# Split fp32r projections in the odd mixer of a two-layer diffusion backbone

## The reference, cut to what matters

```python
z = h @ w_in                                  # h: normed, modulated tokens
ux, ug, up = jnp.split(z, CD_SPLITS, axis=-1) # 512 columns each
zc = hc @ w_in[:, :LRU_W]                     # the context needs ux alone
xl = depthwise_conv(ux, conv_w, conv_b, LRU_PAD)
# for both directions: a, b from sigmoid gates of xl; h_lat += linear_scan(a, b, h0)
lat = [multiscale_pool(up, pool_w, pool_scale), h_lat * gelu(ug)]
x = x + mod[2] * merge_branches(lat, out_norm, w_out)
```

## Time and profile before

| | |
|---|---|
| median of 3 runs | 2559.59 us (2559.36 to 2560.53) |
| profiled execution, its own time | 2562.43 us |
| span of that execution | 2560.6 us |
| PE busy | 2239.7 us, 87% |
| DVE, ACT, POOL busy | 745.8, 606.8, 182.8 us |
| granted PE clock, mean | 0.924 of full speed |
| odd mixer, start of its block to the merge's | 1511.9 to 1788.8 us |
| PE's column sums in its norm (L545) | 1536.45 to 1540.87 us |
| first L490 of ACT in it | 1545.66 us |
| w_out loads of the merge | 4.19 MB, at about 390 GB/s |
| first product of the merge (L1252) | 1805.20 us |

### The profile page before, as it was taken

One profiled execution on the slowest core, in us unless ns is written; L12 is line 12 of the kernel. 1 busy time (PEld: TensorE's weight loads), 2 busy tenths in 40 slices (PEclk: granted clock), 3 DMA queues, 4 the chain that ended last, 5 costly groups with the idle time before them and its releaser, 6 DMA issues. The chain is left out here.

```text
span 2560.6 us, 34982 instructions
## 1 busy us (share of the span) xinstructions
PE 2239.7 (87%) x15176; PEld 1067.3 (42%) x15176; DVE 745.8 (29%) x1167; ACT 606.8 (24%) x960; POOL 182.8 (7%) x126
## 2 busy tenths in 40 slices
PE   4799998969997699999999738998995999988884
PEld 3577885534445233333333224443443333332222
DVE  3423226643114211111111183565315111111104
ACT  4421105541113111111111133554103111111111
POOL 0000000000000000000000021343000000000002
PEclk8799999988998899999999958999897999999986
DMA  8101108035661889889999450000105999999995
GB/s 329 41 25 33 42 2 335 1 91 205 213 214 52 348 358 414 355 346 414 417 415 415 157 180 17 25 25 20 54 1 205 417 415 413 409 419 419 428 427 213
DMA packets 139501, 595.84 MB, mean 233 GB/s; under 512 B 25333, under 2 KB 52689, under 8 KB 114641
## 3 DMA queue, kind: packets, MB, share of 16 engines
q1 hardware_dynamic: 109232, 515.42, 50.6%
q0 software_dynamic: 11952, 43.52, 4.6%
q10 hardware_dynamic: 18160, 34.61, 3.7%
HBM read 534.79 MB, written 58.72 MB: 232 GB/s over the span
## 5 line engine op out<-in xcount | busy, mean ns | idle before, releaser
L1746 PE MATMUL ph<-w,x_t 128*32 128x512 f32 x6016 | 686.7, 610 | 37.6 <-DMA w<-in_exp_w 35.3
L1746 PEld LDWEIGHTS ph<-w,x_t 128*32 128x32 f32 x6016 | 192.7, 112 | 454.1 <-issue 428.6
L1759 PE MATMUL py<-w,g_t 128*32 128x512 f32 x3008 | 341.2, 594 | 1.0 <-DVE g_t L1865 1.0
L1859 DVE TENSOR_TENSOR hidden<-hidden,ph 64x512 f32<-64x512 f32 x94 | 102.3, 1088 | 759.5 <-ACT hidden L1817 759.5
L1252 PE MATMUL z<-Y,w_o 128*128 128x512 f32 (+1 forms) x640 | 258.8, 562 | 0.0
L1817 ACT ACTIVATE hidden<-ph 64x512 f32<-64x512 f32 x94 | 55.5, 590 | 698.8 <-PE ph L1746 698.8
L2071 PE MATMUL z<-hT,w_cd 128*128 128x512 f32 (+1 forms) x448 | 183.3, 567 | 5.7 <-ACT hT L490 5.7
L1759 PEld LDWEIGHTS py<-w,g_t 128*32 128x32 f32 x3008 | 94.0, 110 | 204.6 <-issue 203.3
L706 PE MATMUL z<-h_high,w_hi 128*128 128x512 f32 (+1 forms) x432 | 162.0, 375 | 15.4 <-DVE h_low L538 15.4
L1724 POOL DMA_INDIRECT x_rows<-h_tokens,index x47 | 44.3, 943 | 1821.7 <-PE px L1731 983.3
L1252 PEld LDWEIGHTS z<-Y,w_o 128*128 128x128 f32 x640 | 121.9, 194 | 122.4 <-issue 118.8
(11 more groups left out here) (310 smaller groups left out, 2095.8 us busy)
## 6 DMA issues: line engine op xcount, KB each, us to landing
w<-in_exp_w SPq DMA_DIRECT2D x192, 2048.0 KB, 15.5
ada_raw<-in_ada_w SPq DMA_DIRECT2D x24, 2048.0 KB, 8.6
y_slots<-y_rows ACTq DMA_DIRECT2D x188, 128.0 KB, 9.1
y_slots<-zero SPq DMA_DIRECT2D x29, 512.0 KB, 14.7
h_tokens<-h_rows ACTq DMA_DIRECT2D x18, 512.0 KB, 3.0
w_ab<-in_w_in_ab SPq DMA_DIRECT2D x14, 512.0 KB, 3.8
w_cd<-in_w_in_cd SPq DMA_DIRECT2D x12, 512.0 KB, 3.8
x_t_saved<-xT SPq DMA_DIRECT2D x8, 640.0 KB, 8.9
```

What stands on the lines that cost most here:

```text
L1746: ins = pe.matmul(ph[row:row + UNIT, :], xt[:, k, at:at + UNIT], w13[place[2 * b + n] % RING][:, half, k, :], start=(k == 0), stop=(k == K ...
L1759: ins = pe.matmul(py[b % 2][row:row + UNIT, :], gt[:, k, n * UNIT:(n + 1) * UNIT], w2[place[2 * b + n] % RING][:, k, half * 512:(half + 1) ...
L1859: dve.tensor_tensor(hid[PAIR:P, :].rearrange("s (k q) -> s q k", k=FT), hid[0:PAIR, :].rearrange("s (q k) -> s q k", k=FT), ph[PAIR:P, :]. ...
```

## The change

The odd mixer gets the even mixer's scheme. SP first loads two weight tiles, then saves xT to DRAM (8 issues of 640 KB), then loads the gate and pool weights. The norm is the split one. Each k of a projection is three fp32r products. The weight ring has two places, the low half of a tile lies in the same place as its raw weights, so a load waits until PE has finished with the tile two before. ACT makes the high half of tile m + 1 after the first eviction of tile m; DVE makes the low halves: of tile 2i + 2 after under_root(i - 1, 1) (for group 0 after its convolution), of tile 2i + 3 after under_root(i, 0), of tiles 10 and 11 after the last under_root. When PE has finished the last unit, SP loads the 1024 latent columns of x back into xT (8 issues of 512 KB), and in the merge DVE waits for them ahead of its first eviction. The second pooling buffer is a view of rows 6 and 7 of Y, which ug2 and ug3 fill later.

```diff
--- before.py
+++ after.py
@@ -1341,6 +1341,8 @@
                     ada["chain"] = Chain(dve, ada["step"])
                     self.ada_finish(dve, ada, 0, HERE)
                     dve.engine_nop().then_inc(ada["read"], 1)
+                if layer:
+                    dve.wait_ge(self.s_back, 16 * KT)
                 for n in range(UNITS):
                     c, m = divmod(n, KT)
                     evict(n)
@@ -1977,10 +1979,15 @@
             n = place["ux", i + 1, 2] if later else place["ug", 1, 0]
             pool_at[n] = i
             pool_in[n - 1], pool_in[n] = 2 * i, 2 * i + 1
-        NW = 3
+        NW = 2
         with ExitStack() as ctx:
-            hT = self.sb(ctx, "hT", [P, KT, TOK])
-            w = self.sb(ctx, "w_cd", [P, NW, KT, P])
+            with ExitStack() as same_place:
+                hT = self.sb(same_place, "hT", [P, KT, TOK])
+            h_high = self.sb(ctx, "h_high", [P, KT, TOK], F32R)
+            with ExitStack() as same_place:
+                w = self.sb(same_place, "w_cd", [P, NW, KT, P])
+            w_lo = self.sb(ctx, "w_cd_lo", [P, NW, KT, P], F32R)
+            w_hi = self.sb(ctx, "w_cd_hi", [P, NW, KT, P], F32R)
             gw = self.sb(ctx, "gate_w", [P, 2, 2, BR, P])
             pw = self.sb(ctx, "pool_weights", [P, BR, P])
             up = self.sb(ctx, "u_pad", [P, LRU_ROW])
@@ -1989,11 +1996,13 @@
             sqr = self.sb(ctx, "a_squared", [P, L])
             kept = self.sb(ctx, "lru_total", [P, BR - 1, SEQ])
             total = [kept[:, i, :] for i in range(BR - 1)] + [lanes[0][1][:, 0:SEQ]]
-            pp = [self.sb(ctx, f"pool{n}", [P, PAD + SEQ + PAD]) for n in range(2)]
+            pp = [self.sb(ctx, "pool0", [P, PAD + SEQ + PAD]),
+                  self.Y[:, 2 * BR - 2:2 * BR, :].rearrange("p a n -> p (a n)")[:, 0:PAD + SEQ + PAD]]
             z = [self.ps(ctx, f"z{i}", [P, 512]) for i in range(2)]
             pa, pxg = self.ps(ctx, "pa", [P, 3 * 512]), self.ps(ctx, "pxg", [P, 3 * 512])
             nrm = self.norm_open(ctx, "n1", NT)
             s_w = [self.sem(ctx, f"o_w{i}") for i in range(NW)]
+            s_wh, s_wl, s_saved, self.s_back = (self.sem(ctx, "o_" + n) for n in ("wh", "wl", "saved", "back"))
             (s_sum, s_fwd, s_gw, s_pw, s_zero, s_z, s_ux, s_ug, s_up, s_cv, s_pg, s_r, s_a, s_q, s_sq, s_b, s_h, s_gu, s_y, s_pl, s_pd,
              s_pm, s_pe, s_ch) = (
                 self.sem(ctx, "o_" + n) for n in ("sum", "fwd", "gw", "pw", "zero", "z", "ux", "ug", "up", "cv", "pg", "r", "a", "q", "sqr",
@@ -2002,9 +2011,11 @@
             W = self.i["w_in_cd"][0].rearrange("(k p) n -> p k n", p=P)
             both = ((0, 0, SEQ), (SEQ, GAP, CTX))
 
+            def last_unit(m):
+                kind, i = tiles[m]
+                return place[kind, i, 2 if kind == "ux" else 1]
+
             def wait_z_read(eng, n):
-
-
                 m, i, kind, c = unit[n]
                 if kind == "ux":
                     eng.wait_ge(s_ux, 3 * i + c + 1)
@@ -2015,6 +2026,17 @@
 
             @block.sync
             def _(sp):
+                base = {"ux": 0, "ug": SC_W, "up": 2 * SC_W}
+
+                def load(m):
+                    kind, i = tiles[m]
+                    at = base[kind] + i * P
+                    sp.dma_start(w[:, m % NW, :, :], W[:, :, at:at + P]).then_inc(s_w[m % NW], 16)
+
+                for m in range(NW):
+                    load(m)
+                for k in range(KT):
+                    sp.dma_start(self.xs[:, k, :], self.xT[:, k, :]).then_inc(s_saved, 16)
                 sp.wait_ge(s_zero, 1)
                 for d in range(2):
                     for gate, name in enumerate(("lru_wa", "lru_wx")):
@@ -2022,13 +2044,12 @@
                             sp.dma_start(gw[par * HD:(par + 1) * HD, d, gate, :, par * HD:(par + 1) * HD],
                                          self.i[name][0, d, par::2, :, :].rearrange("i h j -> h i j")).then_inc(s_gw, 16)
                 sp.dma_start(pw[:], self.i["pool_w"][0].rearrange("g i j -> i g j")).then_inc(s_pw, 16)
-                base = {"ux": 0, "ug": SC_W, "up": 2 * SC_W}
-                for m, (kind, i) in enumerate(tiles):
-                    if m >= NW:
-                        before, last = tiles[m - NW]
-                        sp.wait_ge(s_z, place[before, last, 2 if before == "ux" else 1] + 1)
-                    at = base[kind] + i * P
-                    sp.dma_start(w[:, m % NW, :, :], W[:, :, at:at + P]).then_inc(s_w[m % NW], 16)
+                for m in range(NW, len(tiles)):
+                    sp.wait_ge(s_z, last_unit(m - NW) + 1)
+                    load(m)
+                sp.wait_ge(s_z, len(unit))
+                for k in range(KT):
+                    sp.dma_start(self.xT[:, k, 0:SEQ], self.xs[:, k, 0:SEQ]).then_inc(self.s_back, 16)
 
             @block.tensor
             def _(pe):
@@ -2061,15 +2082,17 @@
                 pe.wait_ge(s_pw, 16)
                 for n, (m, i, kind, c) in enumerate(unit):
                     if c == 0:
-                        pe.wait_ge(s_w[m % NW], 16 * (m // NW + 1))
+                        pe.wait_ge(s_wl, m + 1)
                     if n >= 2:
                         wait_z_read(pe, n - 2)
                     at, size = CHUNKS[c]
                     for k in range(KT):
                         if n == 0:
                             pe.wait_ge(nrm["h"], k + 1)
-                        ins = pe.matmul(z[n % 2][:, 0:size], w[:, m % NW, k, :], hT[:, k, at:at + size],
-                                        start=(k == 0), stop=(k == KT - 1))
+                        h_hi, h_lo = (x[:, k, at:at + size] for x in (h_high, self.h_low))
+                        pe.matmul(z[n % 2][:, 0:size], w_hi[:, m % NW, k, :], h_hi, start=(k == 0), stop=False)
+                        pe.matmul(z[n % 2][:, 0:size], w_hi[:, m % NW, k, :], h_lo, start=False, stop=False)
+                        ins = pe.matmul(z[n % 2][:, 0:size], w_lo[:, m % NW, k, :], h_hi, start=False, stop=(k == KT - 1))
                     ins.then_inc(s_z, 1)
                     if n in pool_at:
                         pool_product(pool_at[n], 0, n - 1)
@@ -2080,7 +2103,17 @@
 
             @block.scalar
             def _(act):
-                self.norm_act(act, nrm, hT, 1, 0)
+                def high(m):
+                    act.wait_ge(s_w[m % NW], 16 * (m // NW + 1))
+                    if m >= NW:
+                        act.wait_ge(s_z, last_unit(m - NW) + 1)
+                    act.activation(w_hi[:, m % NW, :, :], w[:, m % NW, :, :], ACT.Copy).then_inc(s_wh, 1)
+
+                def first_tiles():
+                    high(0)
+                    high(1)
+
+                self.norm_act_split(act, nrm, hT, h_high, 1, 0, s_saved, first_tiles)
 
                 def pool_out(i, c, n):
                     act.wait_ge(s_pm, 2 * i + c + 1)
@@ -2134,6 +2167,8 @@
                         if c == 0 and i:
                             act.wait_ge(s_pm, 2 * i)
                         act.activation(pp[0][:, PAD + at:PAD + at + size], z[n % 2][:], ACT.Copy).then_inc(s_up, 1)
+                    if c == 0 and m and m + 1 < len(tiles):
+                        high(m + 1)
                     if n in pool_at:
                         pool_out(pool_at[n], 0, n - 1)
                         pool_out(pool_at[n], 1, n)
@@ -2149,7 +2184,17 @@
                     ins = dve.memset(buf[:], 0.0)
                 ins.then_inc(s_zero, 1)
                 dve.wait_ge(s_zero, 2)
-                self.norm_dve(dve, nrm, hT, z[0], pa)
+
+                def low(m):
+                    dve.wait_ge(s_wh, m + 1)
+                    dve.tensor_tensor(w_lo[:, m % NW, :, :], w[:, m % NW, :, :], w_hi[:, m % NW, :, :].bitcast(F32), ALU.subtract
+                                      ).then_inc(s_wl, 1)
+
+                def first_tiles():
+                    low(0)
+                    low(1)
+
+                self.norm_dve_split(dve, nrm, hT, h_high, z[0], pa, first_tiles)
                 link = Chain(dve, s_h)
 
                 def conv(i):
@@ -2198,11 +2243,16 @@
                     conv(i)
                     if i:
                         under_root(i - 1, 1)
+                    low(2 * i + 2)
+                    if i:
                         scans(i - 1, 1)
                         both_ways(i - 1)
                     under_root(i, 0)
+                    low(2 * i + 3)
                     scans(i, 0)
                 under_root(BR - 1, 1)
+                low(2 * BR + 2)
+                low(2 * BR + 3)
                 scans(BR - 1, 1)
                 both_ways(BR - 1)
                 for i in range(BR):
```

## The result

The changed kernel took 2567.71 us (median of 7 runs, 2564.59 to 2570.07), the kernel before 2558.76 us beside it (7 runs, 2553.14 to 2560.53): ratio 1.0038, 95% interval 1.0026 to 1.0050, or 6.7 to 12.8 us slower. The same kernel once more, against 35 runs of the one before, gave 1.0024 (1.0011 to 1.0037). Forecast was +7.0 us.

A forecast was written before the change was run, and what follows sets the result against it. A ring through POOL, ACT and DVE, not PE, was taken to pace groups 1 to 3. Terms 6.0 + 3.7 + 2.2 - 7.0 + 2.1 = +7.0 us gave 2566.6 us; 8-in-10 range 2560 to 2575.

The forecast's parts named there:

- clock: Groups 1 to 3: PE's clock falls behind longer waits; 0.5 us for groups 1 and 2, 1.7 for group 3.
- Rival (c): Groups 1 to 3: PE does set the pace, so faster projections pay; -18.7 us, 2540.9 us; chance 0.07.
- Rival (b): Mixer's end: SP's loads issue at the saves' pace, w_o's first half becomes the wait; +12 us, 2571.6; chance 0.17.
- Rival (a): Groups 1 to 3: ports hardly meet and PE's clock recovers; +2 us, 2561.7 us; chance 0.16.
- rival (d): Weight tiles arrive late in ug tiles or behind a blocked DVE, some 3 us each; +13, 2573 us; chance 0.04.
- the signs: Odd mixer and merge: predicted eviction time, PE waits, pool-product distances and SP's end, plus observations that would prove it wrong.
- The paragraph on the weight ring: Two-place weight ring: only low(9) is late for ug1, by 2.8 us, hidden before the late pool product 3.
- The front: Start of the odd mixer: split norm's extra ACT and DVE passes delay the third eviction by 11.7 us.
- contention in group 3: Shared DVE/POOL port, group 3: low(9) costs 0.4 us, earlier under_root(3,1) up to 1.5; taken as 1.0.
- the scan fits in front: Group 3: POOL's chain is longer, so DVE's scan fits ahead of it.
- Groups 1 and 2: Ring of POOL, ACT, DVE: contention adds 0.7 us in group 1 and 2.0 in group 2.
- the stretch behind pool product 3: Last five PE units: cheaper products save 7.0 us, against 1.7 lost to the clock in group 3.

The follow-up runs named there:

- The missing product: Changed kernel without the product of high weights with low tokens in the odd mixer's projections: 2562.22 us, ratio 0.9997 to the kernel before.
- back_in_merge: Changed kernel with SP's eight loads of x issued in the merge, behind w_out's loads: 2566.36 us, ratio 1.0025 to the kernel before.
- late_low: Changed kernel with DVE making the low half of tile 2i + 3 after scans(i, 0), groups 0 to 2: 2564.53 us, ratio 1.0014.
- pool_and_back: Changed kernel with DVE's two-input work held back until POOL is through and SP's loads of x moved into the merge: 2552.66 us, ratio 0.9973.
- pool_first: Changed kernel with DVE's under_root, low half and scans waiting for POOL's last operation (group 3: scans only): 2556.38 us, ratio 0.9988.
- the kernel before with POOL first: Kernel before with only DVE's waits for POOL's last operations added, no split products: 2552.06 us, ratio 0.9971; once more 2552.57 us, 0.9970.
- all_three_out: Changed kernel with DVE waiting for POOL, norm by column chunk, x loads in the merge, first two evictions between norm passes: 2548.15 us, ratio 0.9955.

## Why the prediction was right, step by step

| step | forecast, us | measured, us |
|---|---|---|
| third eviction behind the first normalising product | +11.7 | +10.74 |
| first normalising product to pool product 0 | +6.0 | +5.13 |
| pool product 0 to 1 | +0.7 and clock | +0.91 |
| 1 to 2 | +2.0 and clock | +2.14 |
| 2 to 3 | +1.0 | +3.34 |
| 3 to the last eviction | -7.0 + 1.7 | -6.34 |
| last eviction to the merge | +2.1 | +1.86 |
| start of the mixer to the merge | +7.0 | +6.97 |

The mechanism held: PE is not the pace of groups 1 to 3. The missing product is the proof, 10.9 us of the stage (5.8 of the time) where PE as the pace wanted 47.5. Rival (c) had its deciding point in a ring that shortens; it lengthened. Rival (b) failed at its own step: SP's eight loads took 3.88 us and not 9, and behind w_o's loads (back_in_merge) 8.69; the merge's first product came 16.4 us behind its first instruction, as before, so w_o was there in time. Rival (a) is refuted by the distances. Of rival (d) only low(9) came, and under cover.

Of the signs two lay just outside what was named. The third eviction came at 36.90 us (37 to 39 named), PE idled 7.39 and 11.25 us ahead of the products of groups 1 and 2 (6 to 10), the distance 1 to 2 was 50.01 us (48 or more), SP was done 3.9 us after the last eviction began (4). One sign of being wrong, "if PE waits for a weight split", did come by the letter: 2.33 us for low(9) ahead of ug1. The paragraph on the weight ring had forecast it, 2.8 us, hidden in front of the late pool product 3, and so it was.

The front was over by 1.0 us. The first eviction came 28.26 us behind the first normalising product in both mixers, but PE got its full clock back earlier in the second unit, 1.0 us by the evictions (5.76 us between the first two, 6.77 in the even mixer). I had taken the later time over with the even mixer's row. That phase is not fixed: over the runs with this front and all three products it lay between 5.55 (late_low) and 6.85 us (pool_and_back).

The term that was mis-sized is contention in group 3: "low(9) costs 0.4, and an earlier under_root(3,1) may take the port just ahead of L2244, up to 1.5: I take 1.0". The distance grew by 3.34 us, and POOL's operations show where. The fourth window sum took 3.25 us in place of 2.36: 0.9 for low(9). The second of the two edge operations took 1.37 in place of 0.20 and ended with L2217 of under_root(3, 1); the last operation took 3.59 in place of 2.35 behind its L2218: 1.2 each, 2.4 for under_root(3, 1), which went ahead of POOL with both its passes and not with one. The scans cost nothing new there: the scaling (3.89 before, 3.90 after) and the first edge (1.11 in both) were held off before as well, so "the scan fits in front" came true in its effect. That pool_first shortened group 3 by 5.1 us is 2.4 us of under_root(3, 1), 2.0 us of scans, which the kernel before had paid too, and 0.65 of PE's clock in the gates.

Groups 1 and 2 came out as worked, by the mechanism named: in group 2 low(7) cost 0.85 us at the scaling (1.0 forecast) and the long scan 1.86 at the last operation, against 0.4 us of holding before; in group 1 L2226 and the short scan cost 0.9 at the edges (0.7 forecast).

That the sum came out at +6.97 where +7.0 was forecast is luck. Groups 1 to 3 were 2.2 us dearer than the forecast (6.4 against 3.7 and 0.5 of clock). Against it the front was 1.0 too dear, and the stretch behind pool product 3 was 1.0 better: there PE lost 0.7 us more than before and not 1.7 (2.94 us from the first product to the units, 2.71 before with a wait of 0.65 in it, and 27.9 us for five units that take 27.4 at full clock). The remaining 0.2 is the end of the mixer.

No tile other than low(9) was late: a ring of two is enough here. The saves of x, forecast to land at about 1531 us, landed at 1530.9. Behind the mixer 1.0 us came back: the second eviction of the merge is 32.7 us after its start, 33.8 before. That is again the clock and no effect of the change, since the kernel before with POOL first, whose merge is the same, has 33.9 in one profile and 32.6 in the other. The span of the profiled executions grew by 4.9 us only, the medians by 9.0 and 6.7; outside this stage the two profiles differ by 2.1 us the other way, so the whole time confirms the forecast less sharply than the stage does.

## What to carry to other kernels

A cheaper matmul pays only where PE sets the time of a stage; find the ring of waits that does (who releases the engine, and who released that one), and follow it once round, since a speed-up beside it turns into idle time, may start other work early enough to collide, and may slow the engine's own part of the ring when its clock falls behind the longer waits. Where DVE and GpSimd share a stage, put DVE's two-input work behind GpSimd's if GpSimd is on the ring: here two waits gave 7 us to the kernel before, where the rewriting of the projections alone had cost 7 to 9. An operand split that adds two passes for each slice k of the tokens (one on ACT, one on DVE) ahead of the first unit cost 10.7 us at once here, and needs that many saved afterwards.

## What the runs showed of the hardware

POOL's TENSOR_SCALAR does hold DVE off, but only at its start. In the earlier trace rows L2181 began 1.5 us behind it and took its bare 1.50. In the changed kernel L2226 was issued at 1697.94, with the scaling let in at about the same time (it ended at 1700.64, 2.77 before that is 1697.87), and took 2.32: 0.8 us of hold. In late_low the short scan L2229 took 1.40 in place of 0.69 beside a scaling let in at about 1699.5. POOL's TENSOR_TENSOR of 2.34 us held a scan for 2.17, and the other way round a scan of 2.38 us held POOL's L2294 for 1.86.

By the Trainium skill (SBUF — State Buffer, "SBUF: two separate sides" and "Who interferes with whom") a DVE instruction with two SBUF inputs contends with a GpSimd instruction that reads SBUF, and whoever issues first has the shared port pair for the whole instruction. The trace agrees on the meeting of the two, also for the TENSOR_SCALAR, which I had set aside. For this pairing it disagrees on the length: 0.7 to 0.8 us of hold out of 2.77. The rows decide.

PE's clock behind a wait does not follow from the length of the wait. From first to second pool product, with the gates between, PE takes 5.16 to 5.26 us at a granted clock of 1.00, as it does behind a wait of 0.48 us. Behind a wait of 2.00 us in the kernel before with POOL first it took 6.96 us in one profile (granted clock 0.76) and 5.26 in the other (1.00). Behind 4.26 us it took 6.96 in pool_first (0.76), behind 4.27 us 8.11 in all_three_out (0.64), behind 11.25 us 7.44 in the changed kernel (0.70).

A gain of 2 us in front of a stage of this kernel is not safe: in back_in_merge and pool_and_back it was given back by half-clock periods that began or ended 1 us differently.
